# Fourteen sums over a head as four 64x64 products in the four quarters of the array

## The reference

```python
q = rms_norm(q, qn_w); k = rms_norm(k, kn_w)              # mean of squares over a head
kk = kk / max(sqrt(sum(square(kk), axis=-1)), 1e-12)      # sum of squares over a head
mean = mean(y, axis=-1); var = mean(square(y - mean))     # mean over a head
y = (y - mean) * rsqrt(var + GN_EPS)
```

## Time and profile before

| | us |
|---|---|
| median of three runs | 1135.18 |
| the three runs | 1135.18, 1128.86, 1135.43 |
| the profiled execution | 1131.63 |
| its span, first to last instruction | 1129.6 |
| PE busy | 1073.3 (95%) |
| DVE busy | 641.8 (57%) |
| ACT busy | 443.2 (39%) |
| mean granted TensorE clock | 0.989 of full speed |

### The profile page before, as it was taken

One profiled execution on the slowest core, in us unless ns is written; L12 is line 12 of the kernel. 1 busy time (PEld: TensorE's weight loads), 2 busy tenths in 40 slices (PEclk: granted clock), 3 DMA queues, 4 the chain that ended last, 5 costly groups with the idle time before them and its releaser, 6 DMA issues.

```text
span 1129.6 us, 22475 instructions
## 1 busy us (share of the span) xinstructions
PE 1073.3 (95%) x9788; PEld 832.8 (74%) x9788; DVE 641.8 (57%) x1001; ACT 443.2 (39%) x724; POOL 12.1 (1%) x13
## 2 busy tenths in 40 slices
PE   6989997998999999999999998999999999999998
PEld 3767775776687777777777766587888888888887
DVE  4378899946347584758585745755444223444232
ACT  5253464667334642433334123544343112333211
POOL 0000000000000000000000000000000000000000
PEclk8989999999999999999999999999999999999999
DMA  9721222300323210011101040032232232323330
GB/s 363 315 75 50 84 88 85 105 1 2 103 102 131 75 57 21 26 34 39 39 22 39 3 184 7 20 105 91 95 100 96 93 98 88 93 93 96 110 103 28
DMA packets 26160, 94.98 MB, mean 84 GB/s; under 512 B 2896, under 2 KB 3152, under 8 KB 25552
## 3 DMA queue, kind: packets, MB, share of 16 engines
q1 hardware_dynamic: 26064, 93.54, 24.5%
HBM read 89.34 MB, written 4.19 MB: 83 GB/s over the span
## 4 chain that ended last, share of the span: by engine, by line
PE 82%; DVE 10%; ACT 4%; issue 3%; DMA 0%; SPq 0%; ACTq 0%; DVEq 0%
PE psum L784 20%; PE psum L785 19%; PE psum L786 19%; PE psum L794 5%; PE psum L1161 3%; PE psum L958 2%; DVE work L1833 2%; PE psum L915 2%; PE psum L1174 1%; PE psum L994 1%; PE psum L1233 1%; PE psum L1210 1%; PE psum L1129 1%; PE psum L761 1%; PE psum L1253 1%
## 5 line engine op out<-in xcount | busy, mean ns | idle before, releaser
L1889 DVE TENSOR_TENSOR weights_low<-ring,weights_high 128x1024 fp32r<-128x1024 f32 x72 | 88.2, 1225 | 75.1 <-ACT weights_high L1492 75.1
L1492 ACT ACTIVATE weights_high<-ring 128x1024 fp32r<-128x1024 f32 x72 | 75.8, 1053 | 128.3 <-PE psum L786 127.6
L784 PE MATMUL psum<-normed_high,weights_high 128*128 128x512 f32 x256 | 101.6, 397 | 0.1
L786 PE MATMUL psum<-normed_high,weights_low 128*128 128x512 f32 x256 | 101.1, 395 | 0.0
L785 PE MATMUL psum<-normed_low,weights_high 128*128 128x512 f32 x256 | 101.1, 395 | 0.0
L785 PE MATMUL psum<-hidden_low,weights_high 128*128 128x512 f32 x256 | 99.6, 389 | 0.0
L786 PE MATMUL psum<-hidden_high,weights_low 128*128 128x512 f32 x256 | 99.6, 389 | 0.0
L784 PE MATMUL psum<-hidden_high,weights_high 128*128 128x512 f32 x256 | 99.6, 389 | 0.0
L1462 ACT ACTIVATE work<-psum 128x384 f32<-128x384 f32 (+2 forms) x124 | 58.1, 516 | 72.0 <-PE psum L915 27.8
L1833 DVE SCALAR_TENSOR_TENSOR work<-work,small_sb 128x512 f32<-128x512 f32 x116 | 79.8, 744 | 1.5 <-ACT work L1533 1.5
L784 PE MATMUL psum<-pair_normed_high,pair_weights_high 128*128 128x512 f32 x176 | 76.7, 436 | 0.8 <-DVE normed_low L1893 0.8
(11 more groups left out here) (277 smaller groups left out, 2114.2 us busy)
## 6 DMA issues: line engine op xcount, KB each, us to landing
ring<-weights SPq DMA_DIRECT2D x136, 512.0 KB, 3.5
work<-weights SPq DMA_DIRECT2D x10, 512.0 KB, 13.1
residual<-xT SPq DMA_DIRECT2D x4, 512.0 KB, 5.8
mixed<-weights SPq DMA_DIRECT2D x4, 512.0 KB, 4.9
residual_saved<-residual SPq DMA_DIRECT2D x8, 256.0 KB, 4.3
residual<-residual_saved SPq DMA_DIRECT2D x1, 2048.0 KB, 8.3
outT<-residual SPq DMA_DIRECT2D x8, 256.0 KB, 3.3
tables_sb<-tables SPq DMA_DIRECT2D x1, 1280.0 KB, 12.4
```

The lines of the kernel that those rows point to most:

```text
L784: pe.matmul(out, wh, high(k), start=first and n == 0, stop=False)
L786: ins = pe.matmul(out, wl, high(k), start=False, stop=last and n == len(order) - 1)
L1492: act.activation(wsplit(q)[0], room_of(b), ACT.Copy).then_inc(w_high, 1)
L1889: vec.tensor_tensor(low, room_of(b), high.bitcast(F32), ALU.subtract).then_inc(w_low, 1)
```

## The change

Fourteen sums are made another way: `hs0`, `hs2` to `hs5`, `kks_2` to `kks_5`, and `gm_0` to `gm_4`. In place of one matmul of 128x128 weights over 512 tokens there are four of 64x64 weights over 256 tokens, one for each head and half of the tokens, each in its own quarter of the array. The first half of the tokens goes to one bank with the heads on their own partitions, the second half to the bank behind it with the heads exchanged. The reader takes the sum in three parts: 128 partitions x 256 tokens of the first half, and twice 64 partitions x 256 tokens of the second. In the plan these sums take two banks, fixed to 4 and 5 where `aside` gives them, and the result after them starts the turn at the first bank again. `gm_5`, `kks_0`, `kks_1`, the variance sums `gv` and the bonus sums `bon` stay as they are.

```diff
+QUARTER_SUMS = ([f"hs{n}" for n in (0, 2, 3, 4, 5)] + [f"kks_{p}" for p in range(2, NP)]
+                + [f"gm_{p}" for p in range(NP - 1)])
+HEAD_HALF = S // 2
 ...
     def add(*names):
-        o.extend((n, 1, rotation[0]) for n in names)
+        o.extend((n, 1 + (n in QUARTER_SUMS), rotation[0]) for n in names)
 ...
     def aside(*names):
         for n in names:
-            o.append((n, 1, side_banks[0][side[0] % len(side_banks[0])]))
-            side[0] += 1
+            if n in QUARTER_SUMS:
+                o.append((n, 2, side_banks[0][0]))
+                side[0] = 0
+            else:
+                o.append((n, 1, side_banks[0][side[0] % len(side_banks[0])]))
+                side[0] += 1
 ...
+        def head_sum_parts(name):
+            out = by_parity(name)
+            first, second = slice(0, HEAD_HALF), slice(HEAD_HALF, S)
+            return [(slice(0, P), first, out[:, 0, 0:HEAD_HALF])] + [
+                (rows(h), second, out[rows(1 - h), 1, 0:HEAD_HALF]) for h in range(HEADS)]
 ...
+            def quarter_sums(name, src):
+                take(name)
+                out = by_parity(name)
+                for half in range(2):
+                    cols = slice(half * HEAD_HALF, (half + 1) * HEAD_HALF)
+                    for h in range(HEADS):
+                        full_inc(pe.matmul(out[rows((h + half) % 2), half, 0:HEAD_HALF], tab("heads")[rows(h), rows(h)],
+                                           src[rows(h), cols], start=True, stop=True), name)
 ...
             def rms(name, out, w, scale, eps, done):
                 act.wait_ge(*is_full(name))
-                free_inc(act.activation(out, bank(name, w), ACT.Ln, bias=eps, scale=scale), name)
+                if name in QUARTER_SUMS:
+                    for part, cols, sums in head_sum_parts(name):
+                        ins = act.activation(out[part, cols], sums, ACT.Ln, bias=eps, scale=scale)
+                    free_inc(ins, name)
+                else:
+                    free_inc(act.activation(out, bank(name, w), ACT.Ln, bias=eps, scale=scale), name)
 ...
             def least_norm(p):
                 vec.wait_ge(*is_full(f"kks_{p}"))
+                    for part, cols, sums in head_sum_parts(f"kks_{p}"):
+                        ins = vec.tensor_scalar(HR[part, 0, cols], sums, KK_LEAST, None, ALU.max)
 ...
             def gn_centre(p):
                 vec.wait_ge(*is_full(f"gm_{p}"))
+                    for part, cols, sums in head_sum_parts(f"gm_{p}"):
+                        ins = scaled_sum(CAT[part, p, cols], sums, -1.0 / DH, CAT[part, p, cols])
```

More of the change, by code:

```diff
@@ L330, in tiles @@
         return 4
+    if name in QUARTER_SUMS:
+        return 4
     if kind in ("xf", "mv", "wu", "h", "yh") and name.count("_") >= 1 or kind.startswith("y") and kind[1:].isdigit():
@@ L343, in psum_plan @@
         here = at % 8 if pinned is None else at % 8 % 7 if pinned == ROTATE_7 else pinned
+        if here + n > 8:
+            here = 0
         fulls[here] += tiles(name)
@@ L794, in one @@
                 full_inc(pe.matmul(take(name, w), stationary, moving, start=True, stop=True), name)
+            def quarter_sums(name, src):
[6 more added lines that the diff above has]
+                                           src[rows(h), cols], start=True, stop=True), name)
             def head_sums(n, w=S):
                 pe.wait_ge(head_sq, n + 1)
-                one(f"hs{n}", tab("heads"), HS[:, n % 2, 0:w], w)
+                if f"hs{n}" in QUARTER_SUMS:
+                    quarter_sums(f"hs{n}", HS[:, n % 2, :])
+                else:
+                    one(f"hs{n}", tab("heads"), HS[:, n % 2, 0:w], w)
             def rotate(n, name):
@@ L1106, in kk_sum @@
                 pe.wait_ge(kk_sq, p + 1)
-                one(f"kks_{p}", tab("heads"), HS[:, 0, :])
+                if f"kks_{p}" in QUARTER_SUMS:
+                    quarter_sums(f"kks_{p}", HS[:, 0, :])
+                else:
+                    one(f"kks_{p}", tab("heads"), HS[:, 0, :])
             def bonus_sum(p):
@@ L1114, in gn_mean @@
                 pe.wait_ge(*is_free(f"yh_{p}"))
-                one(f"gm_{p}", tab("heads"), CAT[:, p, :])
+                if f"gm_{p}" in QUARTER_SUMS:
+                    quarter_sums(f"gm_{p}", CAT[:, p, :])
+                else:
+                    one(f"gm_{p}", tab("heads"), CAT[:, p, :])
             def gn_square(p):
@@ L2188, in least_norm @@
                 vec.wait_ge(*is_full(f"kks_{p}"))
-                free_inc(vec.tensor_scalar(HR[:, 0, :], bank(f"kks_{p}"), KK_LEAST, None, ALU.max), f"kks_{p}")
+                if f"kks_{p}" in QUARTER_SUMS:
+                    for part, cols, sums in head_sum_parts(f"kks_{p}"):
+                        ins = vec.tensor_scalar(HR[part, 0, cols], sums, KK_LEAST, None, ALU.max)
+                    free_inc(ins, f"kks_{p}")
+                else:
+                    free_inc(vec.tensor_scalar(HR[:, 0, :], bank(f"kks_{p}"), KK_LEAST, None, ALU.max), f"kks_{p}")
             def bonus(p):
@@ L2226, in gn_centre @@
                 vec.wait_ge(*is_full(f"gm_{p}"))
-                free_inc(scaled_sum(CAT[:, p, :], bank(f"gm_{p}"), -1.0 / DH, CAT[:, p, :]), f"gm_{p}")
+                if f"gm_{p}" in QUARTER_SUMS:
+                    for part, cols, sums in head_sum_parts(f"gm_{p}"):
+                        ins = scaled_sum(CAT[part, p, cols], sums, -1.0 / DH, CAT[part, p, cols])
+                    free_inc(ins, f"gm_{p}")
+                else:
+                    free_inc(scaled_sum(CAT[:, p, :], bank(f"gm_{p}"), -1.0 / DH, CAT[:, p, :]), f"gm_{p}")
             def gn_finish(p):
```

## The result

| | us |
|---|---|
| before, median of 8 runs | 1132.54 (1128.86 to 1135.43) |
| after, median of 8 runs | 1138.64 (1136.71 to 1144.83) |
| ratio after / before | 1.0051 [1.003, 1.0071] |
| after, the profiled execution | 1140.54 |
| its span | 1138.8 (before: 1129.6) |

The changed kernel is slower by 0.5%, 5.8 us, with an interval of 3.4 to 8.0 us. Forecast were 1138 us and +4.75 us. The total came out as forecast, but its terms did not: two of the three are nearly twice what was put down for them and the third over three times, and part of that does not show in the time. That the total fits is in part luck.

The account below looks back on a forecast made before the run. PE, busy 95% of the span, was taken as the bound. First block 1.2, four pairs 3.1 and pair 5 0.45 made +4.75 us: 1136.4 on the profiled execution, 1139.9 on the median, middle 1138 us, range 1130 to 1146.

Parts of the forecast that it names:

- The matmuls: On PE, a quarter sum takes 0.43 us; saves 0.62 at a `kks` or `gm`, 0.22 at an `hs`.
- in turn: Rival, chance 0.07: at every sum the four quarters do not fill, 1.71 us a sum; 1151.5 us in all.
- one row tile per bank at a time: Rival, chance 0.09: a half's two products on one bank run one after the other, 0.43 us more per sum; 1141.
- The wait for `r`: At `kks_2` to `kks_5`: the second bank makes PE wait, about 1.3 us each, for DVE's read of `r`.
- The wait for `r` does not decide: Rival, chance 0.13: the four `kks` could start at their old time, so about nothing changes; 1133.5 us.
- `from_state` +0.77: Behind each of the four `kks` on PE, `from_state` starts at 564.84 instead of 564.07, +0.77 us.
- The reads: On DVE, three parts take 0.99 us against 0.60, +0.39, end to end +0.58; on ACT also +0.39 taken.
- A pair: Four pairs, `kks` and the `gm` that follows: `y4` starts 0.78 us later in each, +3.1 us together.
- From here PE is the bound: After `y4` in the four pairs: DVE is as late as PE, so nothing gives the 0.78 us back.
- First block: `hs2` to `hs4`: each longer logarithm delays DVE, then the weights, by 0.39 us; +1.2 us, bounds 0 and 1.8.
- the named price of 0.4 for a cover that is gone: First block, `hs0` and `hs5`: both put at nothing, but 0.4 us each if what covers their longer logarithms is gone.
- Pair 5: `e0` waits until DVE has read `gm_4`, +0.85 us, part absorbed before `y4`: +0.45, bounds 0 and 0.85.

Follow-up runs that it names:

- bank_wait: Kernel before, one full matmul and one read per sum, but `kks_2` to `kks_5` take banks 4 and 5: 1136.87 us, ratio 1.0062.
- kks_banks67: Full change, all fourteen quarter sums, but `kks_2` to `kks_5` in banks 6 and 7, so no wait for `r`: 1135.03 us, ratio 1.0022.
- reads_only: Kernel before, full sums in one bank each, but the fourteen read in three parts (128, 64, 64 partitions by 256 tokens): 1139.29 us, ratio 1.0088.
- reads_in_two: Kernel before, the fourteen sums read in two parts, both of 128 partitions by 256 tokens: 1133.28 us, ratio 0.9986.
- kks_only67: Kernel before with only `kks_2` to `kks_5` as quarter products, in banks 6 and 7 without the wait for `r`: 1133.88 us, ratio 1.0023.
- gm_only: Kernel before with only `gm_0` to `gm_4` as quarter products: 1134.0 us, ratio 0.9997.
- hs_only: Kernel before with only the first block's five `hs` sums as quarter products: 1132.11 us, ratio 0.9981.
- kks_only: Kernel before with only `kks_2` to `kks_5` as quarter products: 1137.83 us, ratio 1.0042.
- diagonal: Kernel before, `kks_2` to `kks_5` and `gm_0` to `gm_4` as two 64x64 products over 512 tokens, one bank, one read: 1128.68 us, ratio 0.9989.
- diagonal_5: The kernel of diagonal unchanged, timed again against the kernel before over more rounds: 1129.42 us, ratio 0.9956.

## Why the prediction was right or wrong

**The matmuls** were sized well for the engine itself. The next product starts 0.45 us after the first record of a sum in a pair, though the eight records span 0.66 us and not the 0.45 to 0.55 forecast. In the stream of the first block:

```profile
130.19 0.66 PE L823 MATMUL psum<-head_squares,tables_sb 64*64 64x256 f32 x8
130.79 1.12 PE L814 MATMUL psum<-weighted,tables_sb 128*128 128x512 f32 x2
```

0.60 us to the next product against 0.85 in the earlier trace rows; put down were 0.43 + 0.20 = 0.63. That ends two rivals: *in turn* wanted 1.71 us a sum, *one row tile per bank at a time* 0.43 more than was put down. The rule of the Trainium skill (TensorEngine Tiling (Array Packing), Gotcha 1: PSUM Pressure) that went with it doesn't hold here for two row tiles that write different partitions of one bank: eight records sit within 0.66 us, and the next product, here on the full array, starts 0.60 us after the first of them.

**The wait for `r`** was right in place and number: four waits of 1.2 us, on the read of `r`, and the sum 0.11 us behind its end. *The wait for `r` does not decide* falls by bank_wait and kks_banks67: the wait alone puts `y4` 1.32 us later, and without it a pair costs 0.35. "`from_state` +0.77" measured +0.70 at the addition.

**The reads** are the mis-sized term. The step was "three parts are 0.99 us against 0.60: +0.39. Laid end to end they would be +0.58". I took DVE's overlap from two reads that start at the same partition and gave it to parts that do not. Measured is +0.71 at `kks` (1.31 to 0.60), +0.59 at `gm` (1.33 to 0.74), and on ACT 1.15 to 0.59, +0.56: the end-to-end bound and a little more. reads_only and reads_in_two show that the change of the start partition does it.

**A pair: +0.78 forecast, +1.46 measured.** The first mask +1.41 and not +1.16 (the read, 0.32 over, less 0.07). `y2` +1.26 and not +1.06. Then `gm` was to give back 0.28 and takes 0.20 more: its read is 0.34 over the 0.99, and the sum saves less there than put down, since from its first record to DVE's read it is 0.78 us (575.90 - 575.12), 0.38 less than the 1.16 of before and not 0.62. "From here PE is the bound", so that nothing gives it back, fits: the four pairs and pair 5 make 4 x 1.46 + 1.53 = 7.4 us, and the trace is 7.16 us longer from the `yh` of pair 0 to that of pair 5. One trace alone would not show it: in kks_only67 the same stretch is 5.8 us longer where its milestones give 0.6, and there the granted clock was 0.50 for 10.2 us (695.7 to 705.9), which it was nowhere in that stretch before. The times at one clock below bear it out better.

**First block: +1.2 forecast, +2.25 measured.** The mechanism was right, DVE late by each longer logarithm and PE's wait for the low weights 0.7 to 2.3 us. The three waits grew by 1.6 us, 0.55 each, not 0.39. The rest is `hs0`, which the prediction put "at nothing". DVE waits for its consequence on the context keys, from its timeline in the kernel after:

```profile
103.14 0.48 DVE L1874 SCALAR_TENSOR_TENSOR work<-psum,small_sb,head_rstd 128x256 f32<-128x256 f32 x1 [0.59 <-ACT head_rstd L1460]
```

The longer logarithm of `hs0` delays `hs1`'s on ACT, and DVE, not PE, is what pays: the named price of 0.4 for a cover that is gone, paid with 0.59.

**Pair 5: +0.45 forecast, +1.53 measured.** The wait of `e0` was forecast at +0.85 with a part of it absorbed:

```profile
682.57 0.67 PE L814 MATMUL psum<-memory_keys_values,work 64*128 64x256 f32 x2 [1.52 <-DVE mixed L1877]
```

Counted from the last chain step, `e0` starts at 10.77 us where it started at 8.90, 1.87 late, and `y4` is 1.53 late. So 0.34 us was absorbed, near the 0.40 put down; what failed is the size of `e0`'s delay. Of the 1.02 us that it is over, 0.32 is the longer read: in gm_only `e0` starts 2.22 us after the sum (673.75 to 675.97) where the prediction had 1.75 + 0.15 = 1.90 and the earlier trace rows 1.05. The rest is idle time of PE ahead of `y2` of the second head:

```profile
680.05 0.39 PE L1200 MATMUL psum<-work 64*64 64x64 f32 x6 [0.69 <-issue]
```

kks_banks67 has the same gap in the same place, before and gm_only have none; what PE waited for there stays open.

The delay from `e0` to `y4` is also where the clock comes in. Busy time from `e0` to `y4` in the kernel after, gm_only and kks_banks67 (columns as in the earlier trace rows; the third value from the end is the granted clock):

```profile
682.60:685.00 2.40, 2.40 (x68) 1.55 (x68) 2.25 (x5) 1.05 (x3) 0.00 (x0) 0.93 1.02 415
676.00:679.10 3.10, 3.10 (x68) 2.01 (x68) 2.25 (x5) 1.05 (x3) 0.00 (x0) 0.70 1.03 422
675.40:678.80 3.40, 3.40 (x68) 2.33 (x68) 2.33 (x5) 1.06 (x3) 0.00 (x0) 0.63 0.99 399
```

The same products take 2.46, 3.14 and 3.45 us. In all three traces the clock falls from full speed to half of it (from 2.4 to 1.2 GHz) within about 2 us of the end of `e0`'s wait of 1.5 us; in the kernel after it does so only as `y4` starts. That makes `y4` 0.68 us later in gm_only and 0.99 in kks_banks67. Whether the wait brings the fall about was not tried.

**The sum.** By these milestones the change should cost 2.25 + 4 x 1.46 + 1.53 = 9.6 us. The ratio says 5.8, at most 8.0. That the forecast of 4.75 was near the result is luck: its terms were 4.9 us too small together, and of what they should have been nearly 4 us does not show in the time (2.8 us at one clock, below).

Much of the scatter of the times is the granted clock. Worked out over the 185 runs on record that list it, a run of a kernel whose mean granted clock is 0.001 lower than another's takes 1.0 us longer; with that taken off, the scatter of the runs of one kernel falls from 3.6 to 1.3 us. The last column takes every run to the clock 0.989 in this way and compares it with the 77 runs of the kernel before that list their clock (plus or minus: 95%). What a change costs by changing the clock is taken out of it too.

| kernel | by milestones | measured | interval | at one clock |
|---|---|---|---|---|
| after | +9.6 | +5.8 | 3.4 to 8.0 | +6.8 ± 0.8 |
| hs_only | +2.3 | -2.2 | -5.6 to 1.2 | +0.2 ± 0.7 |
| kks_only | +5.3 | +4.8 | 0.7 to 8.8 | +5.7 ± 0.7 |
| gm_only | +2.3 | -0.3 | -4.3 to 3.7 | +0.7 ± 0.9 |
| bank_wait | +5.3 | +7.0 | 4.5 to 9.5 | +4.2 ± 2.1 |
| kks_only67 | +0.6 | +2.6 | 0.6 to 4.6 | +1.3 ± 0.8 |
| kks_banks67 | +6.1 | +2.5 | -1.6 to 6.6 | +0.9 ± 0.5 |
| reads_only | +6.2 | +10.0 | 8.1 to 11.9 | +5.4 ± 1.8 |
| reads_in_two | +0.3 | -1.6 | -5.3 to 2.3 | +0.2 ± 1.0 |
| diagonal | -3.3 | -1.2 | -3.4 to 1.0 | -3.7 ± 0.8 |
| diagonal_5 | -3.3 | -5.0 | -8.0 to -1.8 | -2.5 ± 0.7 |

At one clock reads_only no longer costs more than its milestones, and the two timings of the diagonal form agree on a gain of 2.5 to 3.7 us. Without the first block's term, after comes to +7.4 and hs_only to 0, against +6.8 and +0.2. gm_only comes to +1.6 and kks_banks67 to +2.9 when the clock's share in pair 5 is left out too, against +0.7, which its margin nearly covers, and +0.9, which it does not. From the first scores to the `yh` of pair 0, the attention stage takes 271.0 to 272.1 us in the four traces whose `hs` reads are late, 271.6 to 275.1 in the nine others: 1.4 us less on average, with the ranges touching. So it is shown that the first block's 2.3 us do not reach the end in hs_only; by what they are made good, and why kks_banks67 costs 2 us less than its milestones, stays open.

## What to carry to other kernels

A faster product counts only with what its new shape asks of others: count the banks it now holds, and who last reads them, before the columns that it saves. Price a read that is cut up by a row with the same change of the start partition, not by a row with the same number of elements. When two quarters of the array would do, leaving the other two to the neighbours, in one bank and with one read, can be worth more than filling all four: 64x64 on the diagonal gained 0.8 us in a typical pair where the four quarters lost 1.46. And compare times at the same granted clock before a few microseconds are explained: within one kernel's runs it made up most of the scatter.

## What the runs showed that was not expected

- Reads of PSUM that follow each other on DVE overlap when they start at the same partition (0.33 us from one 256-element read to the next, also from 128 to 64 partitions), and don't when the start partition changes (0.42 to 0.45 us; one alone takes 0.42). ACT does the same (steps of 0.26 us against 0.38 to 0.39; 1.15 us for three parts against 0.59 for the whole).
- A fall of the granted clock to half made the same products from `e0` to `y4` take 3.45 us instead of 2.46, in the kernel that was to take a wait away.
- A product of 64x64 on a quarter that a long neighbour leaves free starts beside it, 0.48 to 0.57 us after the start of a sum whose records span 1.03 us, and in one place 0.29 us ahead of a product that stands before it in the program.
